# Score pairs issued ahead of the transposes and value matmuls of their step, in both attention mixers of an encoder trunk

## What is computed

```python
def _forget_core(q, k, v, dq, dk, q_pos, k_pos):
    s = jnp.einsum('bqhd,bkhd->bhqk', q, k).astype(jnp.float32) * ATTN_SCALE
    s = s + jnp.swapaxes(dq, 1, 2)[..., :, None] - jnp.swapaxes(dk, 1, 2)[..., None, :]
    s = jnp.where(k_pos[None, :] <= q_pos[:, None], s, NEG_INF)
    p = jax.nn.softmax(s, axis=-1).astype(v.dtype)
    return jnp.einsum('bhqk,bkhd->bqhd', p, v)
```

## Time and profile before

| what | value |
| --- | --- |
| median of 3 runs | 2719.94 us (2719.84 to 2721.36) |
| the profiled execution's own time | 2712.55 us |
| its span in the profile | 2710.7 us |
| PE busy | 2520.6 us (93%), 18210 instructions |
| VectorE (DVE) busy | 1299.5 us (48%) |
| ScalarE (ACT) busy | 837.2 us (31%) |
| mean granted clock of TensorE | 0.957 |
| chain that ended last | PE 84%, DVE 8%, ACT 4%, DMA 2% |

### The profile page before, as it was taken

One profiled execution on the slowest core, in us unless ns is written; L12 is line 12 of the kernel. 1 busy time (PEld: TensorE's weight loads), 2 busy tenths in 40 slices (PEclk: granted clock), 3 DMA queues, 4 the chain that ended last, 5 costly groups with the idle time before them and its releaser, 6 DMA issues.

```text
span 2710.7 us, 42807 instructions
## 1 busy us (share of the span) xinstructions
PE 2520.6 (93%) x18210; PEld 2283.5 (84%) x18210; DVE 1299.5 (48%) x2126; ACT 837.2 (31%) x1542; POOL 190.7 (7%) x252
## 2 busy tenths in 40 slices
PE   4799999989997999999989999997999888999997
PEld 2599999878885689999959999995888775999997
DVE  1476642445555567433256733326555545333324
ACT  1322222244443232222232222114444423222212
POOL 0100000121110110000020000003111102000000
PEclk8899999989996989999989999997999988999998
DMA  5565542222221345433226533223323222332330
GB/s 135 154 171 160 167 130 86 89 79 72 72 72 46 97 140 172 121 93 100 77 86 179 157 100 101 86 67 93 96 88 96 73 61 89 93 86 86 106 90 34
DMA packets 393222, 277.76 MB, mean 102 GB/s; under 512 B 12128, under 2 KB 349952, under 8 KB 393032
## 3 DMA queue, kind: packets, MB, share of 16 engines
q1 hardware_dynamic: 384248, 253.20, 31.9%
q0 software_dynamic: 8784, 21.82, 2.8%
HBM read 262.04 MB, written 12.93 MB: 101 GB/s over the span
## 4 chain that ended last, share of the span: by engine, by line
PE 84%; DVE 8%; ACT 4%; DMA 2%; issue 1%; POOL 1%; SPq 0%; ACTq 0%; POOLq 0%; DVEq 0%
PE lin L830 70%; PE ps_o L1048 3%; PE ps_s L879 2%; PE ps_s L995 2%; PE ps_t L860 1%; DVE rstd L1499 1%; DMA raw<-in_w_ada 1%; PE ps_t L1016 1%; PE lin L852 1%; DVE x L1530 1%; DVE neg_max L1615 1%; POOL prod L749 1%; DVE y L1523 1%; DVE h_lo L1514 0%; ACT h_hi L1228 0%
## 5 line engine op out<-in xcount | busy, mean ns | idle before, releaser
L830 PE MATMUL lin<-h_hi,w_hi 128*128 128x272 f32 x3600 | 783.9, 299 | 50.5 <-DVE h_lo L1514 41.9
L830 PE MATMUL lin<-h_hi,w_lo 128*128 128x272 f32 x3600 | 755.4, 292 | 0.0
L830 PE MATMUL lin<-h_lo,w_hi 128*128 128x272 f32 x3600 | 753.4, 291 | 0.0
L830 PEld LDWEIGHTS lin<-h_hi,w_hi 128*128 128x128 f32 x3600 | 571.7, 192 | 109.6 <-issue 64.6
L830 PEld LDWEIGHTS lin<-h_lo,w_hi 128*128 128x128 f32 x3600 | 576.9, 192 | 0.0
L830 PEld LDWEIGHTS lin<-h_hi,w_lo 128*128 128x128 f32 x3600 | 573.1, 192 | 0.0
L1438 DVE TENSOR_TENSOR w_lo<-raw,w_hi 128x1024 fp32r<-128x1024 f32 (+1 forms) x260 | 343.6, 1322 | 416.2 <-ACT w_hi L1180 416.1
L1180 ACT ACTIVATE w_hi<-raw 128x1024 fp32r<-128x1024 f32 (+1 forms) x260 | 293.1, 1128 | 173.3 <-PE lin L830 173.3
L830 PE MATMUL lin<-act_hi,w_hi 128*128 128x272 f32 x1408 | 291.7, 288 | 0.0
L830 PE MATMUL lin<-act_hi,w_lo 128*128 128x272 f32 x1408 | 290.6, 288 | 0.0
L830 PE MATMUL lin<-act_lo,w_hi 128*128 128x272 f32 x1408 | 290.5, 288 | 0.0
(11 more groups left out here) (228 smaller groups left out, 2350.7 us busy)
## 6 DMA issues: line engine op xcount, KB each, us to landing
raw<-in_w_ada SPq DMA_DIRECT2D x144, 512.0 KB, 3.7
raw<-in_ffn_w_gate SPq DMA_DIRECT2D x88, 512.0 KB, 3.9
raw<-in_ffn_w_up SPq DMA_DIRECT2D x88, 512.0 KB, 4.2
raw<-in_ffn_w_down SPq DMA_DIRECT2D x64, 704.0 KB, 4.6
raw<-in_w_in_ab SPq DMA_DIRECT2D x24, 512.0 KB, 3.8
raw<-in_w_in_c SPq DMA_DIRECT2D x24, 512.0 KB, 3.8
dk_b<-decay_scratch POOLq DMA_DIRECT2D x16, 400.0 KB, 4.5
out<-k_nat POOLq DMA_DIRECT2D x16, 256.0 KB, 2.6
```

The source lines that it names most:

```text
L830: m = nc.tensor.matmul(lin[:, 2 * out + a, 0:HALF], w[:, hl, k, :], mv[:, a * HALF:(a + 1) * HALF], start=first and n == 0, stop=last and ...
```

## The change

In TensorE's part of a step, the call of the two `scores` moves from the end of the step to the place right behind the projections (`lin_chunk` and `turn_out`), ahead of `transpose_probs` and `values`. The waits inside the functions go with them. Nothing else is changed; the order on the other engines is as before.

```diff
@@ -1068,15 +1068,15 @@
                             turn_out(j // 2)
                     if att is None:
                         continue
+                    if s < 10 and s % 2 == 0:
+                        scores(s)
+                        scores(s + 1)
                     j = s - lag
                     if 0 <= j < 10 and (att != "b" or j % 2):
                         transpose_probs(j, j // 2 if att == "b" else j)
                     j = s - lag - 1
                     if 0 <= j < 10 and (att != "b" or j % 2):
                         values(j, j // 2 if att == "b" else j)
-                    if s < 10 and s % 2 == 0:
-                        scores(s)
-                        scores(s + 1)
 
```

## The result

The changed kernel took 2741.03 us (median, 2739.70 to 2742.33) against 2719.94 us: ratio 1.0076, interval 1.0059 to 1.0094. That is +21.1 us where +13.3 was forecast. The direction held, and so did the mechanism in the stages with projections; the size was low, and 2741.03 lies at the very upper end of the range of 2724 to 2741.

A forecast was written before the change was run, and what follows sets the result against it. Bound by TensorE (projections 70% of the span); 9.6 (a and c) + 1.9 (b) + 1.8 (last stages) = +13.3 us, giving 2733.3 us on the median's scale, 0.5% slower; range 2724 to 2741.

The forecast's parts named there:

- It can't, from step 4 on: take(s-3) stands in front of it: In a and c stages: bias addition starts 0.3 us later, since emptying ps_o stands ahead of it and waits for values.
- Terms of steps 4, 6 and 8: Projection stages of a and c: delays of 0.30, 0.27 and 0.30 us, 0.87 per stage, 9.6 us in all.
- b, +0.64 at the turn of step 9: Projection stages of b, step 8: scores no longer cover ScalarE's emptying of ps_t; +0.64 us each, 1.9 for three.
- The last stages, +1.8: Last b and last c stage, without projections: waits splitting score pairs cost +1.0 and +0.8 us; bounds -2.8 to +5.
- Rival 1: Moved waits meet slack in the same step, only the last stages pay: 0 to +4 us, say 2722; chance 0.14.
- Rival 2: In a and c the bias addition starts some 1.1 us earlier, removing waits: 16 us gained, 2704; chance 0.05.
- Rival 3: Longer waits make TensorE's clock fall in each c stage: 2 us in 7 stages, 14 more, 2747; chance 0.07.
- signs that I had named for being wrong: Bias addition before emptying ps_o; step-5 transposes waiting no longer; last stages shorter; clock below 1.00 in a projection stage.

The follow-up runs named there:

- e3: The changed kernel with, on VectorE in a and c, the emptying of ps_o moved behind the bias addition: 2704.35 us, ratio 0.9943 to the kernel before.
- e4: The kernel before, scores at the end, with only VectorE's emptying of ps_o moved behind the bias addition in a and c: 2722.97 us, ratio 1.0008.
- e8: The kernel before with scores in front and emptying of ps_o behind the bias addition in a and c, b unchanged: 2699.24 us, ratio 0.9926.
- e12: The kernel before with both new orders in a and c, plus five unread matmuls in each of steps 2 to 11 of the last stages: 2692.2 us, ratio 0.9899.
- e10: The kernel before with scores in front only in a set of steps that differs from stage to stage: 2727.59 us in its one execution.
- e1: The changed kernel with the old order kept in the last stage of each mixer: 2734.4 us, ratio 1.0051 to the kernel before.
- e13: The kernel before with five unread matmuls in each of steps 2 to 11 of the two last stages: 2713.62 us, ratio 0.9972.
- e9: The changed kernel with the emptying of ps_o behind the bias addition everywhere, b included: 2705.06 us, ratio 0.9949 to the kernel before.
- e2: The kernel before with the scores in front in the two last stages alone: 2727.27 us, ratio 1.0023.
- e11: The changed kernel with five unread matmuls in each of steps 2 to 11 of the two last stages: 2732.7 us, ratio 1.0053 to the kernel before.

## Why the prediction was right in direction and low in size

- **"It can't, from step 4 on: take(s-3) stands in front of it".** Shown: add(4) directly behind take in the timeline, and in e3 the one edit of VectorE's order turns +21 into -16 us. Terms of steps 4, 6 and 8: 0.30, 0.27, 0.30 forecast, 0.34, 0.34, 0.35 measured; 11 stages, 10.8 against 9.6.
- **b, +0.64 at the turn of step 9.** Measured 0.63, with the wait of 0.56 where it was forecast, and nothing in step 4. That step 6 costs 0.42 by itself was missed: the transposes that add(6) waits for are moved too. The sum came out right only because both delays end in one wait. The forecast's own terms (0.38, 0.37, 0.15 behind 713.84) add up to 714.74, so +0.59, and leave out the 0.11 us between the transposes and probsT in the earlier trace rows; it is the end of that sum that came out, not each part.
- **The last stages, +1.8.** This is the step that failed: "The mean clock is already low there (0.68 in c), so a somewhat longer wait should change little of it". The term measured 8.1 us, beyond its own bound of +5. The working of the waits was fair for the full clock: 1.1 and 1.1 up to the last fillers, 1.87 (b) and 0.83 (c) over the whole filled stages, against 1.0 and 0.8. But it was priced with rows that mostly stand at the full clock. In b the clock is at 0.50 for all but the first 3 to 5 us, with either order (e4 apart), and there the same order costs 2.9. In c the mean of 0.67 was not a floor: it was 1.00 for parts of the stage and 0.50 for others, and with the change it stayed at 0.50 once it had fallen. That is the third rival's mechanism, in the place where I had excluded it. One more wait was overlooked there: in step 2, T(0) stands behind S(3), which waits for add(1) (the 0.80 at 2184.21), and starts 4.51 us behind the first scores instead of 3.86.
- **Rival 1, nothing,** fell by its own test: the waits of T(3) and T(7) grew in every stage. **Rival 2, faster,** named the condition under which it holds, take not in front of add, and the price, 16 us. That 15.9 were measured in e3 is in part luck: the price was for a and c with projections, which gave 20 there, and b took nearly 5 of it back; e8, where b is left out, gave 19.9. **Rival 3, the clock,** didn't come as forecast: the projection stages of c stay at 1.00. It came in the last c stage, and in a smaller form at some borders, below. There one of the signs that I had named for being wrong did appear, a granted clock below 1.00 in a projection stage (0.97 and 0.98 over the four disturbed a and b stages). My argument against it went by the longest gap, 1.6 us in b, and that alone doesn't decide: in the last c stage the clock fell behind idle times of 0.83 and 0.80 us.
- **The total.** It came within the range although one term lay outside its bounds, because the 11 a and c stages and the 3 b stages were forecast well (12.7 us measured, 11.5 forecast). The upper end of 2741 was reached by another sum than the one that it was made of.

## What to carry to other kernels

Issuing a producer earlier gains only as far as the consumer's own queue lets it start: find the instruction ahead of the consumer and what that one waits for, and move both or neither. Where two moved operations delay the same later wait, the larger counts, not the sum; where they end in waits of their own, they add. In a stretch with short waits between short bursts of matmuls, read the granted clock in pieces of a few us and not as a mean: a part at 1.00 can still be lost, and a part at 0.50 makes every delay dearer. A few unread matmuls can be worth much there: in the last c stage they took off 6.0 us (e8 to e12), where the new orders of both engines by themselves left it as long as before (34.62 in e3 and 35.23 in e8, against 34.62).

## What the runs showed of the hardware that was not expected

- **Idle time filled with useless work shortened the chain.** Fifty unread matmuls of 272 columns in a stage took the last c stage from 35.23 us (e8, clock 0.53) to 29.19 (e12, 0.94), and the last b stage of the old order from 40.27 to 37.77.
- **A score pair split by a wait loses its overlap.** Four passes of 384 columns on the two halves of the rows take 0.92 us as one row in e10; two of them, alone behind a wait, take 0.91, at 2184.21 above and at 2182.50, both at a clock of 1.00 (it fell at about 2185.2).
- **Brief falls of the clock between a b stage and the next a stage.** TensorE's windows and timeline at such a border after the change:

```profile
664.00:668.00 4.00, 4.00 (x20) 2.45 (x19) 1.38 (x3) 0.00 (x0) 1.86 (x3) 0.72 0.41 139
```

```profile
664.67 1.88 PE L995 MATMUL ps_s<-kT,qT 64*128 64x512 f32 x4
```

The clock is at 0.72 in this piece, the pair took 1.88 us instead of 1.13, and the two stages that meet there are 0.8 longer each than undisturbed ones (33.35 and 37.54). After the change there are two such pairs of stages, in e1 and in e13 one, and in e9 the a and b stages are uneven from the second on; the traces of before, e2, e3, e4, e8, e10, e11 and e12 have none. e11 has the changed order in these stages and e13 the old one, so the change is neither enough nor needed for it; the cause stays open.
